# GpSimd's share of a chunked delta rule: right-hand sides between the inversion levels, decay masks during the forgetting attention, no selects on the key products

## The reference

```python
gc = jnp.cumsum(g, axis=-1)                         # g: log decay of each token and head
diff = gc[..., :, None] - gc[..., None, :]
decay = jnp.where(incl, jnp.exp(jnp.where(incl, diff, 0.0)), 0.0)        # incl: lower triangle with diagonal
a_mat = jnp.where(strict, einsum("cd,sd->cs", k, k) * decay * beta[..., :, None], 0.0)
rhs = concatenate([v * beta[..., None], k * (beta * exp(gc))[..., None]], axis=-1)
sol = triangular_solve(a_mat + eye, rhs, lower=True, unit_diagonal=True)
u, w = sol[..., :dv], sol[..., dv:]
qk = einsum("cd,sd->cs", q, k) * decay
# per chunk, S is the state:
v_new = u_c - w_c @ S
o_c = (q_c * exp(g_c)) @ S + qk_c @ v_new
S = S * exp(g_last) + (k_c * exp(g_last - g_c)).T @ v_new
```

## Time and profile before

| | us |
|---|---|
| median of three runs | 1144.57 |
| lowest and highest of the three | 1140.43, 1145.12 |
| the profiled execution's own time | 1144.98 |
| its span | 1143.3 |
| TensorE busy | 1023.0 (89%) |
| VectorE busy | 647.6 (57%) |
| ScalarE busy | 461.2 (40%) |
| GpSimd busy | 116.1 (10%) |
| mean granted TensorE clock | 0.91 of 2.4 GHz |

### The profile page before, as it was taken

One profiled execution on the slowest core, in us unless ns is written; L12 is line 12 of the kernel. 1 busy time (PEld: TensorE's weight loads), 2 busy tenths in 40 slices (PEclk: granted clock), 3 DMA queues, 4 the chain that ended last, 5 costly groups with the idle time before them and its releaser, 6 DMA issues.

```text
span 1143.3 us, 16537 instructions
## 1 busy us (share of the span) xinstructions
PE 1023.0 (89%) x6589; PEld 901.3 (79%) x6589; DVE 647.6 (57%) x1003; ACT 461.2 (40%) x747; POOL 116.1 (10%) x109
## 2 busy tenths in 40 slices
PE   3779999997997798899999789999579689999996
PEld 1459899986996586898998689977468569999995
DVE  1466777687547965645544566432744545554554
ACT  2344344444344222544444445542311434443443
POOL 2012011130000000111111100020443000000000
PEclk8889999999997659899999889985679899999999
DMA  9997677876365662255455433620000123555520
GB/s 324 372 387 275 237 256 250 290 268 240 129 234 191 238 221 74 104 192 189 178 204 184 148 132 127 220 74 1 1 1 1 38 74 111 191 176 186 202 89 37
DMA packets 105186, 195.60 MB, mean 171 GB/s; under 512 B 2283, under 2 KB 46572, under 8 KB 105132
## 3 DMA queue, kind: packets, MB, share of 16 engines
q1 hardware_dynamic: 104380, 192.58, 47.7%
q0 software_dynamic: 752, 2.26, 0.6%
HBM read 193.76 MB, written 1.07 MB: 170 GB/s over the span
## 4 chain that ended last, share of the span: by engine, by line
PE 78%; DVE 12%; ACT 3%; DMA 3%; issue 2%; POOL 1%; SPq 0%; DVEq 0%; POOLq 0%; ACTq 0%
PE ps L1686 27%; PE ps L1704 15%; PE ps L1940 7%; PE ps L2148 5%; PE ps L1632 4%; PE ps L1827 4%; DMA raw<-in_w_mod 3%; DVE wl L1072 2%; DVE accu L975 2%; PE ps L2079 1%; ACT arena L585 1%; PE ps L2090 1%; POOL x L450 1%; PE ps L2089 1%; PE ps L1854 1%
## 5 line engine op out<-in xcount | busy, mean ns | idle before, releaser
L1072 DVE TENSOR_TENSOR wl<-raw,wh 128x1024 fp32r<-128x1024 f32 (+1 forms) x288 | 315.5, 1138 | 266.6 <-ACT wh L568 266.6
L568 ACT ACTIVATE wh<-raw 128x1024 fp32r<-128x1024 f32 (+1 forms) x288 | 268.4, 982 | 352.4 <-PE ps L1686 188.1
L1686 PE MATMUL ps<-H,wh 128*128 128x256 f32 x864 | 245.4, 284 | 5.4 <-DVE L L1055 4.4
L1686 PE MATMUL ps<-H,wl 128*128 128x256 f32 x864 | 245.5, 284 | 0.0
L1686 PE MATMUL ps<-L,wh 128*128 128x256 f32 x864 | 245.1, 284 | 0.0
L1686 PEld LDWEIGHTS ps<-H,wh 128*128 128x128 f32 x864 | 166.0, 192 | 9.2 <-issue 8.1
L1686 PEld LDWEIGHTS ps<-L,wh 128*128 128x128 f32 x864 | 166.1, 192 | 0.0
L1686 PEld LDWEIGHTS ps<-H,wl 128*128 128x128 f32 x864 | 165.4, 191 | 0.9
L1704 PE MATMUL ps<-wh,aTh 128*128 128x512 f32 x256 | 101.8, 398 | 1.6 <-DVE wl L1072 1.6
L1704 PE MATMUL ps<-wl,aTh 128*128 128x512 f32 x256 | 101.2, 395 | 0.0
L1704 PE MATMUL ps<-wh,aTl 128*128 128x512 f32 x256 | 101.1, 395 | 0.0
(11 more groups left out here) (378 smaller groups left out, 1716.8 us busy)
## 6 DMA issues: line engine op xcount, KB each, us to landing
raw<-in_w_up SPq DMA_DIRECT2D x16, 2048.0 KB, 8.7
raw<-in_w_down SPq DMA_DIRECT2D x16, 2048.0 KB, 7.7
raw<-in_w_mod SPq DMA_DIRECT2D x12, 2048.0 KB, 16.0
raw<-in_w_in SPq DMA_DIRECT2D x7, 2048.0 KB, 7.7
raw<-in_w_mod SPq DMA_DIRECT2D x12, 1024.0 KB, 7.1
raw<-in_w_qkv SPq DMA_DIRECT2D x6, 2048.0 KB, 11.2
raw<-in_w_mod SPq DMA_DIRECT2D x8, 1536.0 KB, 7.0
raw<-in_w_gate SPq DMA_DIRECT2D x11, 1024.0 KB, 5.3
```

The source lines that it names most:

```text
L568: e.activation(dst, src, ACT.Copy).then_inc(S["split_h"], 1)
L1072: e.tensor_tensor(o, src, i1.bitcast(F32), ALU.subtract).then_inc(S["split_l"], 1)
L1686: ins = e.matmul(ps[:, 4 + b, SEQ * c:SEQ * c + SEQ], w[wb][:, k, P * c:P * c + P], (H, L)[xa][:, k, META:TT], start=(k == 0 and n == 0), ...
```

## The change

- DL and the meta tile's DL wait for the end of the last projection (`split_used`) in place of the norms. In GpSimd's queue they stay behind the multiplication with `gnorm`.
- R1, R1m, Kdm, R2 and Kd are made inside the loop over the levels, behind the level's masks: R1 in level 1, R1m and Kdm in level 2, R2 and Kd of tile 0 in level 3, of tile 1 in level 4. Since X lies over `k_t` by then, R2 and Kd are made from Kb and Kn with the exponentials EG in place of `k_t` with `coef`.
- The selects on AT and ATm are gone: the level masks are zero on and under the diagonal. The selects on PT come after the masks of level 5, and the outputs wait for two `at_p` in place of four.
- TensorE makes the key products in the order AT, AT, meta, PT, PT, and VectorE multiplies them by E_ in that order. Level 0's masks wait for the AT product each.

```diff
@@ gpsimd
             e.wait_ge(S["tk_d"], 8)
-            e.wait_ge(S["nrm_a"], 2)
+            e.wait_ge(S["split_used"], 2 * (T_WIN + 7))
...
-            e.wait_ge(S["gt_a"], 4)
-            e.wait_ge(S["gt_d"], 4)
-            e.wait_ge(S["coef_d"], 3)
...
-            order = [(0, ALU.is_gt), (1, ALU.is_ge), (0, ALU.is_gt), (1, ALU.is_ge)]
-            for i, (which, op) in enumerate(order):
-                e.wait_ge(S["at_d"], i + 1)
-                v = (AT, PT)[which][:, i // 2]
-                e.affine_select(out=v, in_=v, compare_op=op, fill=0.0, base=0, pattern=[[0, GH], [1, P]],
-                                channel_multiplier=-1).then_inc(S["at_p"], 1)
...
+            def right_sides(lv):
+                if lv == 1:
+                    e.wait_ge(S["gt_a"], 4)
+                    e.wait_ge(S["coef_d"], 3)
+                    for m in range(NM):
+                        e.tensor_tensor(R1[:, m], v_t[:, m], bc(beta[:, 1 + m, :], P, P), ALU.mult).then_inc(S["sc_p"], 1)
+                if lv == 2:
...
+                if lv in (3, 4):
+                    m = lv - 3
+                    e.tensor_tensor(R2[:, m], Kb[:, m], bc(EG[:, 1 + m, 0:4], P, P), ALU.mult).then_inc(S["sc_p"], 1)
+                    e.tensor_tensor(Kd[:, m], Kn[:, m], bc(EG[:, 1 + m, 4:8], P, P), ALU.mult).then_inc(S["sc_p"], 1)
             for lv in range(7):
                 for g in groups(lv):
-                    if lv > 1:
+                    if lv == 0:
+                        e.wait_ge(S["at_d"], g + 1)
+                    elif lv > 1:
                         e.wait_ge(S["x_mm"], count(lv - 1, g) + 1)
...
+                if lv == 5:
+                    for m in range(NM):
+                        e.wait_ge(S["at_d"], 4 + m)
...
+                right_sides(lv)
@@ vector
-            for i in range(4):
...
+            def decayed(dst):
+                for i in range(NM):
+                    e.wait_ge(S["kk_mm"], (1 if dst is AT else 4) + i)
+                    e.wait_ge(S["e_set"], i + 1)
+                    e.tensor_tensor(dst[:, i], hv(2 * i + (dst is PT)), E_[:, i], ALU.mult).then_inc(S["at_d"], 1)
+            decayed(AT)
...
+            decayed(PT)
@@ tensor
-            for i in range(4):
+            for i in (0, 2, 4, 1, 3):
...
-                e.wait_ge(S["at_p"], 4)
+                e.wait_ge(S["at_p"], 2)
```

More of the change, by code:

```diff
@@ L513, in _ @@
-            for m in range(NM):
-                e.tensor_tensor(R2[:, m], k_t[:, m], bc(coef[:, 1, 1 + m, :], P, P), ALU.mult).then_inc(S["sc_p"], 1)
-                e.tensor_tensor(Kd[:, m], k_t[:, m], bc(coef[:, 2, 1 + m, :], P, P), ALU.mult).then_inc(S["sc_p"], 1)
-            order = [(0, ALU.is_gt), (1, ALU.is_ge), (0, ALU.is_gt), (1, ALU.is_ge)]
-            for i, (which, op) in enumerate(order):
-                e.wait_ge(S["at_d"], i + 1)
-                v = (AT, PT)[which][:, i // 2]
-                e.affine_select(out=v, in_=v, compare_op=op, fill=0.0, base=0, pattern=[[0, GH], [1, P]],
-                                channel_multiplier=-1).then_inc(S["at_p"], 1)
@@ L524, in _ @@
[L524 to L527, removed]
+            def right_sides(lv):
[5 more added lines that the diff above has]
+                if lv == 2:
+                    e.tensor_tensor(R1m[:, :, :], kv_m[:, 1], bc(beta[0:META, 0, :], META, P), ALU.mult).then_inc(S["sc_p"], 1)
+                    e.tensor_tensor(Kdm[:, :, :], kv_m[:, 0], bc(coef[0:META, 2, 0, :], META, P), ALU.mult).then_inc(S["sc_p"], 1)
+                if lv in (3, 4):
+                    m = lv - 3
+                    e.tensor_tensor(R2[:, m], Kb[:, m], bc(EG[:, 1 + m, 0:4], P, P), ALU.mult).then_inc(S["sc_p"], 1)
+                    e.tensor_tensor(Kd[:, m], Kn[:, m], bc(EG[:, 1 + m, 4:8], P, P), ALU.mult).then_inc(S["sc_p"], 1)
@@ L540, in _ @@
                                         .broadcast_to([META, GH, META]), ALU.mult).then_inc(S["al_p"], 1)
+                if lv == 5:
+                    for m in range(NM):
+                        e.wait_ge(S["at_d"], 4 + m)
+                        e.affine_select(out=PT[:, m], in_=PT[:, m], compare_op=ALU.is_ge, fill=0.0, base=0,
+                                        pattern=[[0, GH], [1, P]], channel_multiplier=-1).then_inc(S["at_p"], 1)
+                right_sides(lv)
         @block.scalar
@@ L1441, in _ @@
             e.tensor_copy(QnT[:, 1], hv(2)).then_inc(S["tt_d"], 1)
-            for i in range(4):
[L1443 to L1446, removed]
+            def decayed(dst):
[4 more added lines that the diff above has]
+            decayed(AT)
+            e.wait_ge(S["kk_mm"], 3)
             e.wait_ge(S["e_set"], 3)
             e.tensor_tensor(ATm[0:META], hv(4, META, META), Em[0:META], ALU.mult).then_inc(S["at_d"], 1)
+            decayed(PT)
             for g in range(3):
@@ L2052, in _ @@
             e.wait_ge(S["tt_a"], 4)
-            for i in range(4):
+            for i in (0, 2, 4, 1, 3):
                 m = i // 2
                 for h in range(GH):
-                    ins = e.matmul(ps[:, i, P * h:P * h + P], KnT[:, m, h, :], (KbT, QnT)[i % 2][:, m, h, :],
-                                   start=True, stop=True)
+                    if i == 4:
+                        ins = e.matmul(ps[0:META, 4, META * h:META * h + META], KnTm[:, h, :], KbTm[:, h, :],
+                                       start=True, stop=True)
+                    else:
+                        ins = e.matmul(ps[:, i, P * h:P * h + P], KnT[:, m, h, :], (KbT, QnT)[i % 2][:, m, h, :],
+                                       start=True, stop=True)
                 ins.then_inc(S["kk_mm"], 1)
-            for h in range(GH):
-                ins = e.matmul(ps[0:META, 4, META * h:META * h + META], KnTm[:, h, :], KbTm[:, h, :], start=True, stop=True)
-            ins.then_inc(S["kk_mm"], 1)
             for g in range(3):
```

## The result

The changed kernel takes 1124.82 us (median of four runs, 1124.33 to 1131.98), against 1144.84 for the kernel before beside it (four runs, 1140.43 to 1146.88). The ratio is 0.9839, 95% interval 0.9807 to 0.987: faster by 1.6%. The profiled execution took 1124.33 us, 20.65 less than that of before. The forecast was 1130 with a range of 1126 to 1138.5. The direction is as forecast, and so are the stretches that gain, but a third of the 20 us lies where nothing was expected.

What follows compares the result with a forecast made beforehand. The preparation was taken to wait on VectorE, stalled beside GpSimd's train of SBUF multiplications, and the levels on TensorE. Gains of 9.3 + 3.0 + 2.3 = 14.6 us from 1144.98 gave 1130 us, range 1126 to 1138.5.

Steps and rivals of the forecast that it cites:

- Part 1: Delta rule's preparation: GpSimd's train of multiplications leaves, so VectorE's scaling multiplications (8.5 us) and a coefficient product (0.8) gain 9.3 us.
- the rule of one instruction at a time: Preparation: VectorE and GpSimd share an SBUF port pair, locked for one whole instruction, the loser blocked; set aside for the trace.
- My use of it: Preparation: by the port rule, the first tile's four VectorE multiplications would pay about 1 us each, 4 us in all.
- Part 2: Key products to first TT_: no AT selects and a new product order end the first TT_ at 5.5 us, gaining 3.0.
- VectorE's order is the limit: Key products: PT products stand ahead of TT_ in VectorE's queue, limiting the gain; first TT_ ends at 5.5 us.
- Part 3: Levels: moved GpSimd multiplications, 2.05 us a level, fit its 3.85 us idle time; cost 0, VectorE's updates undelayed.
- Part 4: Level 1: a shorter TensorE gap keeps the clock at 2.4 GHz, 6.6 us instead of 8.9, gaining 2.3.
- Rival A: From the first transposes on, TensorE's clock is at 2.4 GHz: 1.7 us more gain, 1128.7 us; chance 0.25.
- Rival B: Key products at 1.2 GHz, costing 3.4 us, and level 1 no faster: gain 8.9, 1136.1 us; chance 0.22.
- The sum: Whole kernel: 9.3 + 3.0 + 2.3 = 14.6 us off the profiled 1144.98, giving 1130 us.
- a median can be off by about 2.3: Width of the range: three runs before lie within 4.7 us, so 2.3 was put on either end, 1126 to 1138.5.
- Rival E: Preparation: Kb's 6.68 us is not GpSimd's train, or the stall moves to another VectorE multiplication; 1142 us, chance 0.05.

Runs made afterwards that it cites:

- r1_early: Changed kernel with only R1's two multiplications back in the preparation, right behind the coefficients, the other right-hand sides between the levels; 1139.22 us.
- rights_early: Changed kernel with all eight right-hand sides ahead of the levels again, DL still made in the attention; 1137.89 us.
- dlm_early: Kernel before with only the meta tile's short DL (DLm, 16x64 elements) made in the attention; 1142.04 us.
- t0_first: Changed kernel with VectorE's first TT_ put between the two PT products instead of behind both; ratio to before 0.9879.
- rights_triple: Changed kernel with every right-hand side made three times over, 16 more GpSimd multiplications between the levels; 1143.56 us.
- dl_late: Changed kernel with DL's masks waiting for the key norms again, all else as changed; 1133.6 us.
- part2_only: Changed kernel with DL after the norms and right-hand sides ahead of the levels as before; AT selects gone, new key-product order kept; median 1139.11 us, ratio 0.9944.

## Why the prediction was right, and where it was not

- Part 1, 9.3 us. Kn to the second tile's transposes gave 8.50, as summed, and the coefficient its 0.8; 0.57 of that went back at once, since the transposes to token rows took 4.54 us at 0.50 against 3.97 at 0.59. What was wrong is the reading: I took the stall for what a train does, and put the rule of one instruction at a time aside. Without the short DLm the same train gives turns of 1.45 us and 11.9 us in all. The 8.5 us came out because the very train whose stall had been measured was removed, whatever makes it stall.
- The rule itself (the Trainium skill, SBUF — State Buffer, § SBUF: two separate sides) fits `r1_early`, `rights_early` and most of `dlm_early`: the loser is blocked for one instruction of about 1 us. My use of it (four multiplications, 4 us) has the right size, 4.2 us in five turns in `rights_early`, but no reason for its count: there are ten multiplications, and GpSimd's eight could have met most. It does not explain Kb's 6.7 us, nor the 3.9 us of a GpSimd multiplication in `rights_early` and `dlm_early`.
- Part 2, 3.0 us: measured 3.07, with the first TT_ 5.6 us behind the key products against 5.5. That VectorE's order is the limit held only for the first TT_, as `t0_first` shows.
- Part 3, nothing: held. The updates stayed at 0.69, GpSimd's masks of levels 4 and 5 still waited for TensorE, and `rights_triple` confirms the cover from the other side.
- Part 4, 2.3 us: measured 2.29, with the key products and level 1 granted 1.00. Rival A did not come: the first tile's transposes ran at 0.50. (In `dl_late` the second tile's ran at 1.00 and gave 1.5 us, near A's 1.7.) Rival B's slow key products came in two experiments, at 1.8 and 1.9 us instead of 3.4, since the clock rose within the key products, and level 1 kept its 6.6.
- The sum, 14.6 us: the touched stretches give 14.2. That the ratio puts the time at 1126.1, 0.1 inside the range, is luck: the median is outside it. The step that failed is the width, "a median can be off by about 2.3". Half the spread of three times is no measure where the times come in groups, and the attention alone moved by 8.1 us between the two profiles while the output stage moved by 1.6 the other way. The trace of before had shown an attention at 0.59 and transposes at 0.61, and I applied Part 4's reasoning only to the stages that the change touches. The lowest single time of before that was known, 1140.43, less 14.6 is 1125.8, and less the 16.3 of rival A 1124.1: a range that took single times seriously would have reached down to about 1124.
- Rival E, the change not doing what it says, is excluded by `part2_only`, where Kb's 6.68 us come back with the train.

## What to carry to other kernels

Where two engines have work with both operands in SBUF, read the shortest and the longest instruction of one line, and look for what the other engine runs beside the long one. Its work is best put beside instructions that read PSUM: here they stayed at 0.69 us even with three times the amount beside them. And where a kernel's single times come in groups, compare stretch by stretch on the chain, since a whole stage may run at another clock with nothing changed in it.

## What was not expected of the hardware

- Two engines that both multiply from SBUF take turns in most places (VectorE 1.45 us in place of 0.60, GpSimd 1.48 in place of 1.03), but one may pass the other over for several instructions: a VectorE multiplication took 6.76 us beside six of GpSimd's (three profiles), a GpSimd one 3.9 beside the last four of VectorE's (two profiles). The first came only with a 16x64 instruction of GpSimd's just ahead, the second only without it, and each was the same to 0.02 us wherever it came; why is open.
- The same instructions of the attention took from 31.85 to 23.78 us, at 0.59 to 0.84. Two more products per head cost 0.3 us a head where both run at 1.00 (two heads took 6.10 us with them, 5.50 without), and yet made it 23.0 us in both profiles, at 0.98.
